# Expert stage with one gather for two groups: one-hot fp32r products of split rows, the norm's factor applied per slot

## What is computed

```python
x = x + mixed @ w_out[l]
hn = rmsnorm(x, norm2_w[l])
...
lg = (xt @ wg).astype(jnp.float32) + bg
grp = jnp.argmax(lg, axis=-1)
...
combine = jnp.sum(jax.nn.one_hot(eid, N_EXPERTS, dtype=jnp.float32) * w[..., None], axis=1)
h = jax.nn.silu(jnp.einsum('td,edf->tef', xt, w_gate)) * jnp.einsum('td,edf->tef', xt, w_up)
h = h * combine.astype(h.dtype)[..., None]
y = jnp.einsum('tef,efd->td', h, w_down)
```

## Time and profile before

| | us |
|---|---|
| median of 3 runs | 1044.68 |
| lowest and highest | 1043.57 and 1048.4 |
| span of the profiled execution, first to last instruction | 1042.4 |
| last gate and up tile of the first expert done, TensorE goes on | 434.9 |

### The profile page before, as it was taken

The page is one execution under the profiler, slowest core; times in us unless marked ns, Lnnn a source line. Parts: engine busy times, 40 slices in busy tenths (PEclk is TensorE's granted clock), DMA queues, the critical chain, the costliest instruction groups (busy, mean ns, idle before and its releaser), DMA issues.

```text
span 1042.4 us, 13131 instructions
## 1 busy us (share of the span) xinstructions
PE 1007.5 (97%) x4610; PEld 820.7 (79%) x4610; DVE 745.5 (72%) x647; ACT 601.9 (58%) x562; POOL 5.4 (1%) x21
## 2 busy tenths in 40 slices
PE   5999999998999998999999999999999999999995
PEld 5788888887777787888889788889788889788883
DVE  4654444678666555788884988885988885988884
ACT  6543434338565335577774677764676764677771
POOL 1000000000000000000000000000000000000000
PEclk9999999999999998999999999999999999999999
DMA  9955555555533551599995899995899994899972
GB/s 305 340 204 165 198 165 197 162 162 203 173 110 113 194 160 60 184 360 370 372 368 199 283 357 375 366 367 185 292 365 366 369 369 176 301 362 374 370 279 82
DMA packets 98072, 271.07 MB, mean 260 GB/s; under 512 B 11044, under 2 KB 20856, under 8 KB 97912
## 3 DMA queue, kind: packets, MB, share of 16 engines
q1 hardware_dynamic: 97904, 270.60, 72.9%
q10 hardware_dynamic: 136, 0.04, 0.0%
HBM read 268.51 MB, written 2.10 MB: 260 GB/s over the span
## 4 chain that ended last, share of the span: by engine, by line
PE 92%; DVE 3%; ACT 3%; DMA 1%; issue 0%; SPq 0%; DVEq 0%; ACTq 0%
PE ps L1246 26%; PE ps L1248 26%; PE ps L1247 26%; PE ps L1521 5%; DVE w_lo L708 1%; ACT w_hi L382 1%; PE ps L1343 1%; PE ps L1538 1%; PE ps L1372 1%; PE ps L1552 1%; PE ps L1479 1%; PE ps L1270 1%; PE ps L1539 1%; ACT xT_hi L391 1%; DMA x<-in_x 1%; PE ps L1358 0%
## 5 line engine op out<-in xcount | busy, mean ns | idle before, releaser
L708 DVE TENSOR_TENSOR w_lo<-raw,w_hi 128x2048 fp32r<-128x2048 f32 x251 | 574.1, 2292 | 171.1 <-ACT w_hi L382 170.2
L382 ACT ACTIVATE w_hi<-raw 128x2048 fp32r<-128x2048 f32 x251 | 480.7, 1918 | 201.8 <-PE ps L1248 198.8
L1246 PE MATMUL ps<-w_hi,xg_hi 128*128 128x512 f32 x512 | 205.3, 401 | 0.0
L1247 PE MATMUL ps<-w_lo,xg_hi 128*128 128x512 f32 x512 | 202.3, 395 | 0.0
L1248 PE MATMUL ps<-w_hi,xg_lo 128*128 128x512 f32 x512 | 202.2, 395 | 0.0
L1246 PE MATMUL ps<-w_hi,xT_hi 128*128 128x512 f32 x288 | 115.1, 400 | 2.8 <-DVE w_lo L726 2.6
L1248 PEld LDWEIGHTS ps<-w_hi,xg_lo 128*128 128x128 f32 x512 | 96.0, 187 | 23.6
L1247 PE MATMUL ps<-w_lo,xT_hi 128*128 128x512 f32 x288 | 114.4, 397 | 0.0
L1248 PE MATMUL ps<-w_hi,xT_lo 128*128 128x512 f32 x288 | 114.3, 397 | 0.0
L1246 PEld LDWEIGHTS ps<-w_hi,xg_hi 128*128 128x128 f32 x512 | 96.4, 188 | 21.8
L1247 PEld LDWEIGHTS ps<-w_lo,xg_hi 128*128 128x128 f32 x512 | 96.2, 188 | 21.7
(11 more groups left out here) (235 smaller groups left out, 846.3 us busy)
## 6 DMA issues: line engine op xcount, KB each, us to landing
raw<-in_exp_w_gate SPq DMA_DIRECT2D x128, 512.0 KB, 5.0
raw<-in_exp_w_up SPq DMA_DIRECT2D x128, 512.0 KB, 6.3
raw<-in_exp_w_down SPq DMA_DIRECT2D x128, 512.0 KB, 5.5
raw<-in_w_in SPq DMA_DIRECT2D x36, 1024.0 KB, 5.1
raw<-in_w_out SPq DMA_DIRECT2D x16, 1024.0 KB, 5.3
raw<-in_cmp_w_k SPq DMA_DIRECT2D x4, 1024.0 KB, 6.7
raw<-in_cmp_w_v SPq DMA_DIRECT2D x4, 1024.0 KB, 5.4
x<-in_x SPq DMA_DIRECT2D x4, 512.0 KB, 6.2
```

Of the source, the lines that this page charges most:

```text
L382: act.activation(w_hi[:, slot, :], raw[:, rslot, :], ACT.Copy).then_inc(hi_ready, 1)
L708: dve.tensor_tensor(w_lo[:, slot, :], raw[:, rslot, :], w_hi[:, slot, :].bitcast(F32), ALU.subtract).then_inc(lo_ready, 1)
L1246: pe.matmul(dst, l_hi, r_hi, start=start, stop=False, skip_group_check=True)
L1247: pe.matmul(dst, l_hi, r_lo, start=False, stop=False, skip_group_check=True)
```

## The change

- `hn` is no longer made. DVE writes x1 times `norm2_w` without the norm's factor into `x1w`, laid out by feature chunk, so that 128 features of a chunk lie side by side; ACT copies it to `hn_hi` and DVE subtracts into `hn_lo`, both fp32r, block by block in the output projection. ACT's two scalings of `hn` go.
- `sel` has 256 columns, for two groups, and is fp32r. `gather(m, r)` forms two feature chunks for both groups in a round: four matmuls of 256 columns with `hn_hi` into one PSUM bank, four with `hn_lo` into another. ACT copies the one to `xg_hi`, DVE copies the other to `xg_lo`. A pair has eight rounds, and there are two pairs.
- The norm's factor is gathered with the shares (`cmb9`, nine columns), as a scale on SiLU's input and as a factor in the shares.
- The hand-written order becomes one sequence of steps over 32 experts: four `gate_up` tiles of one expert, then two `down` tiles of the expert before, across group ends too. A group's eight scatters stand in its successor's second and third expert. The second pair's gather stands in the last expert of group 1. The first expert's order on ACT and DVE is new, and part of the router's work (`top_two`) stands later.

Core of the diff:

```diff
-                for c in range(4):
+            def gather(m, r, bank_hi=5, bank_lo=6):
+
+                for bank, src, done in ((bank_hi, hn_hi, gathhi_done), (bank_lo, hn_lo, gathlo_done)):
+                    for k in range(2):
+                        for t in range(TT):
+                            ins = pe.matmul(ps[:, bank, 2 * P * k:2 * P * k + 2 * P], src[:, t, 2 * r + k, :], sel[:, t, :],
+                                            start=(t == 0), stop=(t == 1))
+                    ins.then_inc(done, 1)
...
-                        ins = pe.matmul(ps[:, 5 + r % 2, P * c:P * c + P], hn[:, t, 4 * r + c::KC], sel[:, t, :],
-                                        start=(t == 0), stop=(t == 1))
-                ins.then_inc(gather_done, 1)
```

On ACT the first expert, and the splits ahead of the expert stage:

```diff
+            def x1w_hi(b):
+                act.wait_ge(x1w_ready, b + 1)
+                cs = slice(32 * b, 32 * b + 32)
+                act.activation(hn_hi[:, :, :, cs], x1w[:, :, :, cs], ACT.Copy).then_inc(hnhi_ready, 1)
...
-            for t in range(TT):
-                act.activation(hn[:, t, :], hn[:, t, :], ACT.Copy, scale=st[:, 58 + t:59 + t]).then_inc(hn_ready, 1)
+            x1w_hi(3)
...
+            def first_step(x, m, p0, router=False):
+
+                gathered(m, 0, 5)
+                gathered(m, 1, 0)
+                gathered(m, 2, 5)
                 if router:
                     router_exps()
...
+                gathered(m, 3, 0)
+                gathered(m, 4, 5)
+                moe_hi(p0 + 3)
+                gathered(m, 5, 0)
+                gathered(m, 6, 5)
+                gathered(m, 7, 0)
+                act.wait_ge(share_ready, m + 1)
+                silu(x, 0, p0 + 3)
```

On DVE the layout of `x1w`, and a step:

```diff
+                dve.tensor_tensor(x1w[:, :, :, 32 * b:32 * b + 32].rearrange("p t c m -> p t m c"),
+                                  x1[:, :, cs].rearrange("p t (m c) -> p t m c", c=KC),
+                                  over(norm2b[:, cs].rearrange("p (m c) -> p m c", c=KC), 1, [P, TT, 32, KC]),
+                                  ALU.mult).then_inc(x1w_ready, 1)
...
                 x1_add(b)
+                if b:
+                    x1w_lo(b - 1)
...
+            def next_step(x, g, p0, gather=None, gathering=None, boundary=False, adding=None, turned=None):
+
+                moe_lo(p0)
+                if gathering is not None:
+                    gathered(gathering, 4, 6)
+                    gathered(gathering, 5, 6)
+                    gathered(gathering, 6, 6)
+                moe_lo(p0 + 1)
...
+                hT_evac(x - 1)
+                if adding is not None and adding > 0:
+                    add_back(g - 1, 4 * adding - 2)
+                    add_back(g - 1, 4 * adding - 1)
+                if turned is not None:
+                    take_selT(turned)
...
+                for c in range(4):
+                    if boundary:
+                        yg_evac(g - 1, c)
+                    if gather is not None and c >= 2:
+                        gathered(gather, c - 2, 6)
+                    moe_lo(p0 + 2 + c)
```

On TensorE the step with the second pair's rounds:

```diff
+            def next_step(x, g, p0, start=False, gather_next=None, gathered=None, scat=None, turn=None):
...
+                    gate_up(p0 + c4, 4 + c4, c4, g % 2)
...
+                    if gather_next is not None:
+                        if c4 == 0:
+                            pe.wait_ge(sel_ready, gather_next + 1)
+                            pe.wait_ge(scat_added, 8 * (2 * gather_next - 1))
+                        else:
+                            pe.wait_ge(xghi_ready, 8 * gather_next + c4)
+                            pe.wait_ge(xglo_ready, 8 * gather_next + c4)
+                        gather(gather_next, c4)
```

More of the change, by code:

```diff
@@ L65 @@
 T_MOE = T_OUT + N_OUT
-PER_GRP = 6 * EPG
+N_MAIN = 6 * NEXP
 LEAD = SPL
@@ L125, in layer_kernel @@
         region.n = 0
-        ((xT_hi, xT_lo), (blk_hi, blk_lo, prob, pT_sb), (_, x1T, junk), (hn, xg_hi, xg_lo)) = region(
+        ((xT_hi, xT_lo), (blk_hi, blk_lo, prob, pT_sb), (x1w, hn_hi), (hn_lo,)) = region(
             32768,
@@ L1032, in _ @@
             dve.sem_inc(onehot_ready, 1)
-            for t in range(TT):
-                step(dve.tensor_tensor(prod[:, t], le[:, t], over(Gm[:, t, 0:4], 2, [P, 4, 8]), ALU.mult))
-            step(dve.tensor_reduce(leg, prod.rearrange("p t g e -> p t e g"), AX, ALU.add))
+            x1w_lo(3)
             dve.wait_ge(rank_done, 1)
@@ L1091, in make_sel @@
+            shares = rt[:, 480:496]
+            def make_sel(m, halves=2):
                 for t in range(TT):
-                    ins = dve.tensor_scalar(sel[:, t, :], iota[:, :], rcol[:, t:t + 1], gcol[:, t:t + 1],
-                                            ALU.is_equal, ALU.mult)
+                    for h in range(halves):
+                        k = 2 * m + h
+                        ins = dve.tensor_scalar(sel[:, t, P * h:P * h + P], iota[:, :], rank[:, t, k:k + 1], Gm[:, t, k:k + 1],
+                                                ALU.is_equal, ALU.mult)
@@ L1225, in _, with last_group @@
-            make_sel(0)
-            first_expert(0, between=((top_two,), (lambda: lo(T_MOE + LEAD - 1),), (count_tokens,), (expert_weights,)))
-            make_sel(1)
-            with dve.Fori(0, NGRP - 1) as q:
-                other_experts(q, True)
-            other_experts(NGRP - 1, False)
+                            hT_evac(x0 + e - 1)
+                    h_mul(x0 + e, g)
+            def last_group(x, g, tiles):
+                moe_lo(tiles - 2)
+                moe_lo(tiles - 1)
+                hT_evac(x)
+                yg_evac(g, 0)
+                yg_evac(g, 1)
+                for k in range(4):
+                    add_back(g, k)
+                yg_evac(g, 2)
+                yg_evac(g, 3)
+                for k in range(4, 8):
+                    add_back(g, k)
@@ L1525, in transpose_sel, with take_shares @@
-            def transpose_sel():
-                for t in range(TT):
-                    ins = pe.transpose(ps[:, 5, P * t:P * t + P], sel[:, t, :], ident[:, :])
+            def take_shares(m):
+                pe.wait_ge(sel_ready, m + 1)
+                for h in range(2):
+                    for t in range(TT):
+                        ins = pe.matmul(ps[:, 7, S + 16 * h:S + 16 * h + 9], sel[:, t, P * h:P * h + P].bitcast(F32),
+                                        cmb9[:, t, :], start=(t == 0), stop=(t == 1))
+                ins.then_inc(share_done, 1)
```

642 lines of the change are left out of this document (316 added, 326 removed).

## The result

| | us | ratio to before, with 95% interval |
|---|---|---|
| before | 1044.12 (1043.46 to 1048.4, 4 runs) | |
| changed | 1022.16 (1019.56 to 1022.83, 4 runs) | 0.9776 [0.9753, 0.9799] |
| changed, run again (e9) | 1019.33 (1016.63 to 1021.8, 5 runs), before 1046.07 | 0.9755 [0.9736, 0.9774] |
| six edits on top of the change (e10) | 1005.61 (1003.62 to 1006.41, 5 runs), before 1046.07 | 0.9613 [0.9594, 0.9631] |

By the medians the change makes the kernel 22 us faster, and 27 us in the second set of runs (e9); by the ratios, which use the means, it is 23 to 26. The forecast was -29.6, to 1015. The profiled span went from 1042.4 to 1021.1 us, -21.3.

A forecast was written before the change was run, and what follows sets the result against it. TensorE's matmul stream was taken to bound the kernel. Terms -41.9 + 7.7 + 4.2 + 1.6 - 1.8 - 0.4 - 0.3 = -30.9, and +1.3 at the start, gave -29.6: 1015 us, forecast 1007 to 1020 (0.66), wider range to 1028.

The forecast's parts named there:

- first pair: First gather up to the restart behind the first expert: +1.3 us net, with 2.5 us either way.
- rival (1): Evacuation waits reach 14 us instead of 4.2, or first pair 2.5 us later; about 1023 us, chance 0.15.
- The gather's price: New gather: load and stream overlap, 0.12 us a matmul, 0.96 a round, 7.7 us for a pair of groups.
- rival (2): Gather's weight load and stream add up at 256 columns, +12.8 us less a little; 1027 us, chance 0.12.
- The waits of the second pair: Gather inside expert 15: rounds 1, 3, 5 and expert 16's first tile wait for evacuations or splits, 4.2 us.
- shares and transposes: Expert stage: shares and transposes are needed for pairs of groups instead of each group, -0.4 us.
- Boundaries: Experts after a group end: DVE's added work costs nothing, or 0.5 us at each of three; old waits go, -1.8.
- Rival (3): Load stream falls short without the gathers' rests; slower than before, 1080 us at 300 GB/s, chance 0.035.
- Start of the gather: First pair: `x1w_lo(2)` +1.2, `x1w_lo(3)` 0.1, `make_sel` +0.6 us; start at 408.8 instead of 406.94.
- Restart: TensorE after the first expert: tile 4's split waits behind the first SiLU; 435.7 instead of 434.86 us.
- The clock after the restart: Behind the first expert: 0.5 us set aside because a wait of some 4 us may cost the clock again.
- The end: Last expert: ACT splits the last tile before waiting for transposes, DVE's `hT_lo` behind that split; -0.3 us.

The follow-up runs named there:

- e9: The changed kernel itself, unaltered, run again beside e10 and e11; 1019.33 us, ratio 0.9755.
- e10: e8 with the token count moved ahead of the eighth expert and seven unused matmuls ahead of the first hidden transposes; 1005.61 us, ratio 0.9613.
- e1: Kernel before with only `hn` laid out by feature chunk, still 256 float32 gather matmuls of 128 columns; 1024.08 us, ratio 0.98.
- e11: Changed kernel with `x1w`, `hn_hi` and `hn_lo` laid out by token row again, so the gather's stationary is strided; 1028.4 us, ratio 0.9828.
- e3: Changed kernel with DVE's last `x1w` product moved behind the copy to `x1T` on which the last router logits wait; 1016.63 us, ratio 0.9734.
- e4: Changed kernel plus 8, 6 and 8 unused 512-column matmuls in three TensorE waits between last x1 block and first gather; 1018.58 us, ratio 0.9753.
- e6: Changed kernel with the `sel` transposes two tiles later and DVE's copy of them behind that expert's product; 1017.21 us, ratio 0.9723.
- e7: Changed kernel with four reorderings: splits before SiLU, `x1w` behind `x1T` copy, DVE's gather copies before subtractions, later `sel` transposes; 1008.92 us, ratio 0.9645.
- e8: e7 plus 6, 6 and 8 unused 512-column matmuls in the router's waits; 1006.76 us, ratio 0.9625.
- e2: Changed kernel with ACT's splits of tiles 4 and 5 ahead of the first SiLU and DVE's tile 4 ahead of the shares; 1017.87 us, ratio 0.9744.

## Why the forecast was right in the main and short at the first pair

**The number.** The median of 1022.16 lies outside the 1007 to 1020 that I gave the forecast itself and next to the 1023 of rival (1); e9's 1019.33 lies inside. So the way and the main step are right, and the time is right only within the wider range of 1007 to 1028. A small part of the sum was off as well: a run is 1.7 us longer than its own span (1022.83 for 1021.1), and the 2.3 us that I took compared a span with the median of other executions.

**What bounds the kernel: right.** TensorE's stream set the time. Plain experts take 17.04 us in every one of these kernels, so that whatever left the stream left the span.

**The gather's price: right.** 0.12 us a matmul, on the side of the overlap; 128 x 0.12 = 15.4 us for both pairs. Load and stream don't add up: rival (2) wanted rounds of 1.75 us, and they take 0.95. The reason given, the stride, is shown from both sides, by e1 and e11. The load of 188 ns is 189 to 192 once the clock is kept up (e10).

The Trainium skill (TensorE: Matmul & The Clock Gate, Part 3) would have it that a load overlaps only a matmul in another row group; here, with full 128x128 operands throughout, 0.12 us for a pair whose load alone takes 188 to 192 ns says otherwise. The Trainium skill (SBUF — State Buffer, Door 1: The DMA port swizzle) lets fp32 be strided for free up to 4 elements and no further. The runs agree at 16, with 311 to 317 ns for 188 to 200; no run here has a stride of 4 or less. The price of a strided write, 1.99 us for 1.22, goes the same way.

**The waits of the second pair: right in sum, in part by luck.** Experts 15 and 16 take 21.48 and 25.06 us, 12.5 us above two plain ones; 7.7 + 4.2 = 11.9 was forecast for the gather and its waits. But of the four waits walked through, only two came: rounds 1 and 3 waited 1.33 and 1.31 us (forecast 1.2 and 1.15), round 5 waited 0.24 in place of 1.2, and the first tile of expert 16 didn't wait for its split at all. The waits are 2.9 us in place of 4.2, and what fills the sum up is the eight products with the shares (0.96 us busy), which the forecast had in its term for shares and transposes, and the slower start behind each wait. The wait of the `sel` transposes was forecast at 1.6 and took 1.5.

**Boundaries: right.** The experts with scatters take 18.90 us, that is 17.04 and 8 x 0.233 = 1.86. So nothing of the 0.6 us of other waits in the old period is left, and the DVE work behind a boundary is hidden.

**Loads: right.** Rival (3) needed a stream that falls short without rests. The plain stretches of the changed kernel show 0.94 to 1.00 of the DMA engines' time, the one with the second pair's gather 0.86; TensorE's list of waits names no load, and ACT's splits of the expert stage waited for TensorE alone:

```profile
622.00:639.00 17.00, 17.00 (x75) 13.73 (x74) 14.48 (x8) 12.16 (x9) 0.00 (x0) 1.00 0.94 341
...
843.00:860.00 17.00, 17.00 (x76) 13.70 (x75) 14.45 (x9) 12.11 (x9) 0.00 (x0) 1.00 1.00 373
```

**The first pair: the term that was mis-sized.** I wrote +1.3. From the third block's transposes to the fourth SiLU it is +7.3 in the first profile and +5.5 in e9 (95.49 for 90.04). By its parts, of which the first two are times counted from the transposes, so that the second contains the first:

- Start of the gather, forecast +1.9: +3.6, and +2.75 in e9. The subtraction was priced right (1.22), but I took `x1w` at the price of `hn`. It is written with a stride and takes 1.91 there, 0.7 us more, ahead of the copy on which the logits wait. And I priced the delay, not what a longer wait does to the clock: half clock for the logits costs 1.65 us in the first profile and 0.8 in e9. e3 and e4 show both.
- Restart, forecast +0.84: +4.1 (48.64 for 44.53, from the transposes), and +2.6 in e9. The walk along the queues was right in its order, but it started 1.75 us too early (0.9 in e9) and was itself 1.5 us too short (0.9). Its first step alone, the 24 gather matmuls, took 5.2 us (4.6) where 4.2 were forecast: I had given half clock to 16 of them, and it lasted longer.
- The clock after the restart, 0.5 set aside: 9 matmuls at 0.43 in place of 0.233 are 1.8 us, 7 or so in e9 1.5. The earlier trace rows have the clock at half behind the router's shorter waits, while behind the 1.84 us ahead of the second expert it had stayed at 1.00. No row told which it would be here, so the term needed a range up to the whole price and not a single 0.5.
- Experts 2 and 3: 17.95 and 17.46 us, together 1.3 above plain, forecast 0. In the second stands the count of tokens, 2.1 us in eleven small DVE operations ahead of a split (457.48 to 459.61 us). The forecast has no term for it. DVE has 2.6 us free in a plain expert, but in pieces between splits; 2.1 us in one piece cost 0.9 at both places where it was tried (e10). In the third stand the four transposes of `sel`, which TensorE does without a wait:

```profile
479.24 0.60 PE L1552 MATMUL ps<-ident,sel 128*128 128x128 f32 x4
```

They cost the 0.42 us. It isn't DVE's copy of them: e6, e7, e8 and e10 have that copy behind the expert's product, and expert 3 still takes 17.46 to 17.48. The forecast had the transposes in its term for shares and transposes, which the table above books in the next stretch.

The rest of the miss, 3.4 us, is the front part, which differs from run to run and belonged in the range, not in the sum. e9's profile, which has none of it and is of its shortest run, gives a span of 1014.9 us for the 1012.8 that I wrote: 4.15 more at the first pair, 1.3 less at the end, 0.5 less between, and 0.2 less in front.

**The end.** Forecast -0.3, measured -0.8 to -1.6 (26.5 to 27.3 us from the last SiLU, where before had 28.1). The last scatters' part differs by 0.8 us between runs of the same code: in the first profile the clock fell to 0.50 from 1013 us on, in its last products.

**Rival (1)** had the right place, the first pair, with 2.5 us; it was larger, and the evacuation waits of its other half didn't come.

## What to carry to other kernels

Price a stationary operand by its layout first: here one contiguous layout was worth 20.9 us alone, more than the 17.7 us (e11) of halving the matmuls, fp32r and a new order together, and the two don't add. When a layout moves a stride from a read to a write, the write pays, and it must not stand ahead of what the critical chain waits for. Wherever an edit makes TensorE wait longer, price the wait once as time, and give what follows a range from full to half clock; and ask of a run of small vector operations whether it fits between two splits, whatever the engine has free on average.

## What the runs showed of the hardware

- A strided weight load (16 words apart) takes 311 to 317 ns, for float32 and for fp32r, at 128 and at 256 columns; contiguous it takes 188 to 200. A 256-column fp32r matmul with a full 128x128 stationary starts every 0.12 us, a 128-column float32 one every 0.115.
- DVE writes 1024 float32 elements (for each partition) with a stride of 128 words in 1.91 to 2.01 us and contiguously in 1.22.
- The strided float32 gather hardly felt half clock (7.24 for 7.08 us, with the clock at 0.50 for the first 3 us of it), and the strided fp32r one of e11 only a little (first 24 matmuls at 0.50: 0.23 us each for 0.21); the contiguous one does, 5.39 us for 3.27.
- A wait of 1.84 us was followed by full clock (before, 434 us) and one of 1.71 by half clock (e2) at the same place; the same 1.41 us wait at 345 to 347 us by either.
- Idle matmuls in waits of 1 to 2.4 us keep the granted clock at 1.00, and three such places are worth 2.3 us here (e8 against e7), a fourth 1.4 (e10, expert 1).
- One kernel's runs on a single core spread over 6 us, part of it from stretches at half clock at one place that come in some executions and not in others. A place in the program that both kernels reach with the same code is a better zero than the start of the span.
